# First convolution tap of the state-space input on ScalarE, rotary angles and sines of the differential attention made beside the first FFN

## The reference, cut to what matters

```
z, xbc, dt_raw, q, k, v = split_cols(h @ w_in, EVEN_SIZES)
# Mamba2 group
xbc = silu(causal_depthwise_conv(xbc, conv_w, conv_b))     # 4 taps, 1536 channels
xs, bs, cs = split_cols(xbc, (1024, 256, 256))
dt = softplus(dt_raw + dt_bias);  a = -exp(a_log)
y = ssd_chunked_scan(xs, dt, a, bs, cs) + d_skip * xs
y = rms_norm(y * silu(z), gate_norm)
# differential attention
inv_freq = 10000 ** (-arange(half) * 2 / d);  ang = pos * inv_freq     # d = 64
rotated = [x1 * cos(ang) - x2 * sin(ang), x2 * cos(ang) + x1 * sin(ang)]   # for q and k
```

## Time and profile before

| | us |
|---|---|
| median of 3 runs (lowest to highest) | 2726.69 (2720.05 to 2731.51) |
| the profiled execution | 2719.96 |
| span of its instructions | 2718.2 |
| PE busy | 2572.1 (95%) |
| DVE busy | 1305.1 (48%) |
| ACT busy | 878.3 (32%) |
| POOL busy | 1074.5 (40%) |

### The profile page before, as it was taken

How to read it: one execution, slowest core, us unless ns; L and a number is a source line. 1 busy time by engine, 2 the same in 40 slices (tenths; PEclk the granted TensorE clock), 3 DMA queues, 4 the chain that set the end, 5 groups by cost and what they waited for, 6 DMA issues and landing times.

```text
span 2718.2 us, 30446 instructions
## 1 busy us (share of the span) xinstructions
PE 2572.1 (95%) x11830; PEld 2022.0 (74%) x11830; DVE 1305.1 (48%) x2013; ACT 878.3 (32%) x1354; POOL 1074.5 (40%) x841
## 2 busy tenths in 40 slices
PE   7999999999999999989988999999997789999998
PEld 6878676888788888766766677888885666788886
DVE  4225677533433321585756654585126765533301
ACT  3443245322222222224444533322233243322221
POOL 4322243644454445343222235454452331544442
PEclk9999999999999999999999999999997889999999
DMA  3111122222222223211111122222320011222232
GB/s 134 66 55 63 50 74 72 95 97 94 93 90 95 95 90 94 92 62 60 49 47 47 47 70 99 93 93 91 97 97 30 21 40 39 97 94 94 93 94 74
DMA packets 62575, 209.45 MB, mean 77 GB/s; under 512 B 6880, under 2 KB 9312, under 8 KB 62304
## 3 DMA queue, kind: packets, MB, share of 16 engines
q1 hardware_dynamic: 61424, 204.11, 23.0%
q10 hardware_dynamic: 1008, 3.40, 0.3%
HBM read 205.38 MB, written 2.10 MB: 76 GB/s over the span
## 4 chain that ended last, share of the span: by engine, by line
PE 78%; DVE 14%; ACT 4%; issue 2%; POOL 1%; DMA 0%; DVEq 0%; ACTq 0%; SPq 0%; POOLq 0%
PE ps L609 22%; PE ps L610 22%; PE ps L611 22%; DVE T L2012 1%; PE ps L630 1%; ACT A L1475 1%; PE ps L632 1%; PE ps L631 1%; DVE A L2311 1%; DVE small L2157 1%; PE ps L920 1%; DVE A L1901 1%; POOL w_lo L567 1%; PE ps L737 1%; PE ps L739 1%
## 5 line engine op out<-in xcount | busy, mean ns | idle before, releaser
L567 POOL TENSOR_TENSOR w_lo<-w_raw,w_hi 128x512 fp32r<-128x512 f32 (+4 forms) x822 | 1047.1, 1298 | 1578.2 <-ACT w_hi L1214 1578.2
L609 PE MATMUL ps<-H,w_hi 128*128 128x512 f32 x1880 | 765.4, 407 | 39.5 <-POOL w_lo L567 19.6
L610 PE MATMUL ps<-H,w_hi 128*128 128x512 f32 x1880 | 750.7, 399 | 0.0
L611 PE MATMUL ps<-H,w_lo 128*128 128x512 f32 x1880 | 750.4, 399 | 0.0
L1214 ACT CAST w_hi<-w_raw 128x1024 fp32r<-128x1024 f32 (+4 forms) x411 | 401.9, 983 | 540.7 <-DMA w_raw<-in_weights_dram 535.1
L609 PEld LDWEIGHTS ps<-H,w_hi 128*128 128x128 f32 x1880 | 358.4, 191 | 139.2 <-issue 37.3
L609 PE MATMUL ps<-split,w_hi 128*128 128x512 f32 x1034 | 419.2, 405 | 11.8 <-POOL w_lo L567 5.8
L611 PEld LDWEIGHTS ps<-H,w_lo 128*128 128x128 f32 x1880 | 357.4, 190 | 87.2
L610 PEld LDWEIGHTS ps<-H,w_hi 128*128 128x128 f32 x1880 | 358.5, 191 | 81.9 <-issue 1.4
L610 PE MATMUL ps<-split,w_hi 128*128 128x512 f32 x1034 | 412.5, 399 | 0.0
L611 PE MATMUL ps<-split,w_lo 128*128 128x512 f32 x1034 | 412.1, 399 | 0.0
(11 more groups left out here) (395 smaller groups left out, 2493.7 us busy)
## 6 DMA issues: line engine op xcount, KB each, us to landing
w_raw<-in_weights_dram SPq DMA_DIRECT2D x323, 512.0 KB, 3.6
w_raw<-in_weights_dram SPq DMA_DIRECT2D x48, 448.0 KB, 3.2
w_raw<-in_weights_dram SPq DMA_DIRECT2D x22, 256.0 KB, 2.6
X<-in_xt_dram SPq DMA_DIRECT2D x4, 512.0 KB, 7.6
out_dram<-A SPq DMA_DIRECT2D x8, 256.0 KB, 2.2
w_raw<-in_weights_dram SPq DMA_DIRECT2D x12, 128.0 KB, 2.0
w_raw<-in_weights_dram SPq DMA_DIRECT2D x6, 192.0 KB, 2.3
A<-in_w_gates_dram ACTq DMA_DIRECT2D x1, 1024.0 KB, 5.6
```

Of the source, the lines that this page charges most:

```text
L567: sub = nc.gpsimd.tensor_tensor(w_lo[:, p % NS, c], w_raw[:, p % NS, c], w_hi[:, p % NS, c].bitcast(F32), ALU.subtract)
L609: mm_(ps[:, bank, :], r(wh), xh, start=(k == 0), stop=False)
L610: mm_(ps[:, bank, :], r(wh), xl, start=False, stop=False)
L611: mm = mm_(ps[:, bank, :], r(wl), xh, start=False, stop=(k == kt - 1))
```

## The change

Three edits. First, tap 3 of the convolution (weight times input plus bias) is done by ACT as an Identity activation with a per-partition scale and bias, `last_tap(t)`; it waits for a new semaphore s_xb that DVE gives after each L1728, and gives s_tap, for which `conv_tile` waits instead of s_xs. Second, DVE's order is shifted by one: input of t, then conv_tile(t - 1), then two steps of step_sizes. Third, the angles are computed on DVE beside FFN 1 (two instructions after pair 2, six after pair 6, the cosine's two after pair 18) and the sines on ACT after pair 15; the functions `angles`, `reduce_angle` and `cosine` only move up.

```diff
-            ffn(1, "mix2")
+            def rope_sines(j):
+                if j == 15:
+                    act.wait_ge(s_ang, 1)
+                    link(A_(SIN, ANG, ACT.Sin))
+                    A_(COS, ANG, ACT.Sin, scale=0.5).then_inc(s_sin, 1)
+
+            ffn(1, "mix2", rope_sines)
...
+            def last_tap(t):
+                act.wait_ge(s_xb, t + 1)
+                link(A_(T[:, t % 2, :], XB[:, t, CONV_PAD:], ACT.Identity, scale=vec("ev_conv_w", 36 + t),
+                        bias=vec("ev_conv_b", t)))
+                act.sem_inc(s_tap, 1)
+
+            last_tap(0)
+            last_tap(1)
             for t in range(12):
                 hi_to(last_panel("xbc", t) + 4)
                 act.wait_ge(s_cv, t + 1)
-                A_(XB[:, t, CONV_PAD:], T[:, t % 2, :], ACT.Silu).then_inc(s_xs, 1)
+                link(A_(XB[:, t, CONV_PAD:], T[:, t % 2, :], ACT.Silu))
+                act.sem_inc(s_xs, 1)
+                if t + 2 < 12:
+                    last_tap(t + 2)
                 hi_to(last_panel("xbc", t) + 5)
...
-                if t == 3:
-                    act.wait_ge(s_ang, 1)
-                    link(A_(SIN, ANG, ACT.Sin))
-                    A_(COS, ANG, ACT.Sin, scale=0.5).then_inc(s_sin, 1)
...
+            def rope_angles():
+
+                dve.wait_ge(s_pos, 16)
+                link(v.tensor_copy(ANG2, POS.bitcast(I32)))
+                link(v.tensor_scalar(ANG2, ANG2, con("freq64"), None, ALU.mult))
+                yield
+                reduce_angle(ANG, ANG2, POS)
+                dve.sem_inc(s_ang, 1)
+                for _ in range(11):
+                    yield
+                dve.wait_ge(s_sin, 1)
+                cosine(COS)
+
+            ffn(1, "mix2", lambda k: ("norm_mix_2", k), rope_angles())
...
+            def conv_input(t):
+                scaled_out("xbc", t, XB[:, t, CONV_PAD:])
+                dve.sem_inc(s_xb, 1)
+
             def conv_tile(t):
-                if t >= 2:
-                    dve.wait_ge(s_xs, t - 1)
                 o = T[:, t % 2, :]
-                link(v.tensor_scalar(o, XB[:, t, CONV_PAD:], vec("ev_conv_w", 36 + t), vec("ev_conv_b", t),
-                                     ALU.mult, ALU.add))
+                dve.wait_ge(s_tap, t + 1)
                 for k in (2, 1, 0):
...
-            scaled_out("xbc", 0, XB[:, 0, CONV_PAD:])
-            scaled_out("xbc", 1, XB[:, 1, CONV_PAD:])
+            conv_input(0)
+            conv_input(1)
...
             conv_tile(0)
-            conv_tile(1)
...
             for t in range(2, 12):
-                scaled_out("xbc", t, XB[:, t, CONV_PAD:])
-                conv_tile(t)
+                conv_input(t)
+                conv_tile(t - 1)
                 run(sizes, 2)
+            conv_tile(11)
             run(sizes, 100)
...
             for t in range(8):
                 silu_input(t)
-                if t == 1:
-                    angles(POS, con("freq64"), ANG, ANG2, 16)
-                    dve.sem_inc(s_ang, 1)
                 times_dt(t)
                 if t == 5:
-                    dve.wait_ge(s_sin, 1)
-                    cosine(COS)
                     link(v.tensor_tensor(COS, COS, R, ALU.mult))
```

More of the change, by code:

```diff
@@ L475, in build @@
                                              sem("dt_columns"))
-        s_cv, s_xs, s_xt, s_xtf, s_bc, s_bcf = (sem("conv_ready"), sem("silu_x_ready"), sem("x_turned"),
+        s_xb, s_tap, s_cv, s_xs, s_xt, s_xtf, s_bc, s_bcf = (sem("xbc_ready"), sem("last_tap_ready"), sem("conv_ready"), sem("silu_x_ready"), sem("x_turned"),
                                                 sem("x_turned_read"), sem("bc_ready"), sem("bc_read"))
@@ L1993, in _, with angles, reduce_angle, cosine @@
             dve.sem_inc(s_par, 1)
-            ffn(1, "mix2", lambda k: ("norm_mix_2", k))
+            def angles(pos, freq, out_, a, loaded):
+                dve.wait_ge(s_pos, loaded)
+                link(v.tensor_copy(a, pos.bitcast(I32)))
+                link(v.tensor_scalar(a, a, freq, None, ALU.mult))
+                reduce_angle(out_, a, pos)
+            def reduce_angle(out_, a, whole):
+                link(v.tensor_scalar(whole, a, 1.0 / TWO_PI, MAGIC, ALU.mult, ALU.add))
+                link(v.tensor_scalar(whole, whole, MAGIC, None, ALU.subtract))
+                link(v.scalar_tensor_tensor(out_, whole, -C1, a, ALU.mult, ALU.add))
+                link(v.scalar_tensor_tensor(out_, whole, -C2, out_, ALU.mult, ALU.add))
+                link(v.scalar_tensor_tensor(out_, whole, -C3, out_, ALU.mult, ALU.add))
+                link(v.tensor_scalar(out_, out_, float(np.float32(np.pi)), -float(np.float32(np.pi)), ALU.min, ALU.max))
+            def cosine(c):
+                link(v.tensor_tensor(c, c, c, ALU.mult))
+                link(v.tensor_scalar(c, c, -2.0, 1.0, ALU.mult, ALU.add))
+            def rope_angles():
[10 more added lines that the diff above has]
+            ffn(1, "mix2", lambda k: ("norm_mix_2", k), rope_angles())
             dve.wait_ge(s_parx, 1)
@@ L2061, in _ @@
             dve.sem_inc(s_dtn, 1)
[L2063 to L2080, removed]
             def silu_input(t):
```

## The result

Changed kernel: 2734.18 us, median of 20 runs (2727.05 to 2736.78). Kernel before, on the same chip: 2722.96, median of 20 (2719.61 to 2732.41). Ratio of times 1.003, 95% interval 1.0019 to 1.0041: a little slower, inside the 0.5% that were called no change. The forecast was 2730.0 in 2716 to 2743. The profiled execution took 2734.76 (span 2733.0), 14.8 us more than the one before; the forecast of a profiled execution was 2725.4.

What follows compares the result with a forecast made beforehand. PE holds 78% of the span but gets xbc panels at DVE's pace. z 7 ending 2.7 us later plus 2.7 for lower clock gave 5.4; 2724.6 + 5.4 = 2730.0 us, range 2716 to 2743.

Steps and rivals of the forecast that it cites:

- Sines and angles: Moved from stage z to beside FFN 1: no cost there (bounds 0 to 9 us), gain in z at most 1.1.
- Start of stage xbc: First tap queues on ACT behind Abs, table load and Exp; DVE's next instructions start at 1122.5, 2.8 us late.
- The cast of panel xbc 5: On ACT behind tile 3's tap: input 3 at 1134.0, cast 1135.6, PE starts 1140.1 after 9 us idle.
- DVE's period: Stage xbc, tiles 3 to 5: POOL hits two series instructions, 7.24 becomes 7.4 us; three later periods 0.76 shorter each.
- xbc 11 on PE: Starts from DVE's input 9 (1181.9) at 1188.9, 12.5 us later than before; PE then has its panels in time.
- Clock: PE idles some 4.2 us ahead of xbc 11, which then runs at the lower clock: price 2.7 us, bounds 0 to 2.7.
- Sum: End of z 7 2.7 us later, plus 2.7 for the lower clock: 5.4 us later in all.
- Rival A: DVE sets the end and PE follows without a late panel: 13.4 us less, 2711; chance 0.07.
- B: Stage xbc: POOL and DVE miss each other, period 6.65 us, xbc 11 at 1185.9, total 2724.3; chance 0.15.
- C: The lower clock does not come on PE: total 2727.3; chance 0.2, with neighbours of the POOL-and-DVE-miss case.
- D: PE stays at 1.2 GHz through the stage, tiles 9.8 us, 17 us more: total 2744; chance 0.08.
- E: Identity is not in SiLU's table, so each tap brings ACT two table loads of 1.28 us: total 2733; chance 0.03.

Runs made afterwards that it cites:

- e2: Kernel before with only the angles and sines moved beside FFN 1: median 2724.42 us, ratio to the kernel before 0.9995 to 1.0013.
- e1: Changed kernel with ACT's cast of the next weight panel moved ahead of its tap: median 2727.86 us, ratio to the kernel before 1.0010 to 1.0029.
- e4: Changed kernel with unread matmuls filling PE's idle time ahead of six xbc panels: median 2733.73 us, ratio to the kernel before 1.0031 to 1.0055.
- e3: Changed kernel with angles and sines back in stage z, tap still on ACT: median 2734.81 us, ratio to the kernel before 1.0032 to 1.0054.
- e6: Kernel before with angles beside FFN 1 and ACT's casts ahead of its convolution wait: median 2729.40 us, ratio to the kernel before 0.9997 to 1.0019.

## Why the prediction was right, and where it was off

By its own steps, with 0.5 us taken off the times of the trace after for the later start of its stage:

- *Sines and angles.* Nothing in FFN 1: PE busy 278.83 of 280.00 us from 720 to 1000 as before. Gain at most 1.1 forecast, 1.3 in e2: right in kind, 0.2 more.
- *Start of stage xbc.* DVE's first convolution starts at 1122.64, forecast 1122.5 (2.8 later than before; its idle time of 3.45 also covers the place of the tap that went). The tap takes 0.82 and not 0.72. The table load and Exp are as long as they were.
- *The cast of panel xbc 5.* Input 3 at 1134.26 (1134.0 forecast), cast 1136.06 (1135.6), xbc 5 on PE 1140.45 (1140.1) after 9.29 us idle (9). The mechanism that carries the sum is right, and e1 shows it by taking it away.
- *DVE's period.* Two hits instead of one, as forecast; 7.54, 7.60 and 7.58 against 7.4. Two numbers in 7.24 - 0.58 + 0.75 were too good. The added hit costs 0.83 to 0.86. And the tap's going saves 0.49: from the start of an input to that of its three taps it is 1.42 before and 0.93 after, as the pause between them grew from 0.15 to 0.24. The three later periods are 8.37, 8.57 and 9.29, shorter by 0.53, 0.51 and 0.69 than before, where 0.76 was taken, more than the tap's 0.58 and without a row behind it. Together 1.05 us; with the 0.3 of input 3, input 9 is at 1183.2, forecast 1181.9. This is the term of DVE's sum that was mis-sized: +1.05.
- *xbc 11 on PE.* 7.03 us after input 9 (6.95 forecast), so 1190.2 instead of 1188.9. Then no wait for w_lo in stage z, as forecast.
- *Clock.* It fell on xbc 11, as forecast, but for seven matmuls of 0.63 and one of 0.52 and not for the whole tile: 7.3 us for it instead of 5.65, price 1.65 and not 2.7. It had already fallen on xbc 10, so this ended late (1188.1) and the idle time ahead of xbc 11 was 2.58 and not 4.2; e4 shows that of the earlier falls nothing remains at z 7.
- *Sum.* 0.3 more from input 3, 1.05 more from the period, 1.05 less from the clock and 0.4 more in the steps of z: 6.1 instead of 5.4 in the stage, and z 7 ends at 1249.4, just past the 1246 to 1249 that were given as a sign. The close sum owes something to luck, since two errors of 1.05 us cancel.

Rival A needed the cast of xbc 5 before 1127; it came at 1136.5. B (POOL and DVE miss each other) is out by the rows of the period. C (no lower clock) is out, though what it would have saved is 1.65. D: the clock is 0.93 over 1142 to 1204, 0.94 before. E: between the SiLUs of the tiles and the taps there is no table load; the one at 1124.07 is the first SiLU's, behind Exp. F: see FFN 1.

What the prediction did not have is the later part. It had 2724.6 + 5.4 = 2730.0. The medians differ by 11.2 us, and the stage explains some 6 of them. That 2734.18 lies in the range of 2716 to 2743 is owed to the mechanism for those, and for the rest to a range that had a whole scatter of executions in it. The low group of executions after (2727.0 to 2729.7) is 7 to 8 us above the low group before, not far above the stage's 6.1; the median after lies in the high group. Why the changed kernel is in it in twelve of twenty is open. e3, with late casts too, is at 2731.08 to 2738.99 in five of six, and e2, without them, has one of eleven at 2731.92 and the others below 2726.1; so late casts may make the high group more frequent, which no run here tests.

## What to carry to other kernels

An instruction moved to an idle engine takes with it the wait that it brings: on an engine with one order, ask what stands behind it and who waits for that. Here 0.8 us of tap ahead of a cast cost the stage 6 us, behind it nothing. Taking a tap of 0.55 us off DVE made its period 0.3 longer (7.24 to 7.58), because the second engine's work moved relative to it and hit two instructions instead of one; taking PE's waits away without taking work from DVE only moves them (e6). Where executions of one kernel differ by 12 us, compare the stage in the traces as well as the medians.

## What was not expected of the hardware

- The clock fell on xbc 11 after 2.00 us of idleness with PE kept busier than ever (e4), and on xbc 10 after 2.37 (after), and did not after 3.23 (xbc 11 before): how long PE idled just ahead does not alone tell it. Later in the kernel such stretches add steps of 2.0 and 2.65 us, in executions of several of the kernels, whatever was edited.
- ACT's Identity with two operands by partition takes 0.82 us, 0.10 over L1541's 722 ns with one. The Trainium skill, "ScalarE: Activation LUTs", section "What ACT_TABLE_LOAD costs", has about 93 ns for each such operand; the trace agrees.
- POOL's subtraction lengthens a DVE instruction of 0.42 us with one SBUF input at least as much as one of 0.69 with two: 0.95 against 0.83.
